# Routing by rank in a hybrid attention and mixture-of-experts layer: a shorter choice, moved splits, and reordered gathers and scatters

## The reference, cut to what matters

```python
g_prob = softmax(xt @ w_group + b_group)
g_w, g_idx = top_k(g_prob, 1)                      # one group per token
e_logits = take_along_axis(e_logits_all, g_idx)    # the 4 experts of that group
e_w, e_idx = top_k(softmax(e_logits), 2)           # two of them
e_w = e_w / sum(e_w)
w_tok = g_w[:, None] * e_w
for e in range(16):
    h = silu(xt @ w_gate[e]) * (xt @ w_up[e])
    y = y + combine[:, e:e + 1] * (h @ w_down[e])
x = layer_norm(ALPHA * x + y)
```

## Time and profile before

| | |
|---|---|
| median of 3 runs | 615.74 us (615.70 to 617.25) |
| profiled execution | 615.53 us |
| its span in the trace | 613.6 us |
| PE busy | 591.4 us (96%) |
| DVE busy | 478.5 us (78%) |
| ACT busy | 373.4 us (61%) |
| POOL busy | 129.3 us (21%) |
| share of PE in the chain that ended last | 92% |

### The profile page before, as it was taken

One profiled execution on the slowest core, in us unless ns is written; L12 is line 12 of the kernel. 1 busy time (PEld: TensorE's weight loads), 2 busy tenths in 40 slices (PEclk: granted clock), 3 DMA queues, 4 the chain that ended last, 5 costly groups with the idle time before them and its releaser, 6 DMA issues.

```text
span 613.6 us, 9635 instructions
## 1 busy us (share of the span) xinstructions
PE 591.4 (96%) x3627; PEld 475.8 (78%) x3627; DVE 478.5 (78%) x572; ACT 373.4 (61%) x401; POOL 129.3 (21%) x111
## 2 busy tenths in 40 slices
PE   8999999999999999999799999999999999999991
PEld 6878888888788668877588888888888888888880
DVE  3748598794577775546898989888888988888967
ACT  3659434431315984213478877877877787787745
POOL 0004222290000340000484443111110111111010
PEclk9999999999999999999899999999999999999997
DMA  9821133223306003975699999999999999999754
GB/s 325 299 98 57 63 130 111 95 71 78 72 1 206 2 2 125 422 271 211 239 375 420 404 363 389 392 388 391 409 404 389 389 389 389 399 410 397 269 172 137
DMA packets 42573, 155.77 MB, mean 254 GB/s; under 512 B 11955, under 2 KB 12163, under 8 KB 30252
## 3 DMA queue, kind: packets, MB, share of 16 engines
q1 hardware_dynamic: 37516, 138.40, 57.8%
q0 software_dynamic: 5024, 16.92, 10.6%
HBM read 139.96 MB, written 15.34 MB: 253 GB/s over the span
## 4 chain that ended last, share of the span: by engine, by line
PE 92%; DVE 4%; issue 1%; ACT 1%; DMA 1%; DVEq 0%; SPq 0%
PE psum L673 26%; PE psum L675 25%; PE psum L674 25%; PE psum L1072 2%; PE psum L791 2%; PE psum L931 2%; PE psum L908 2%; PE psum L1089 1%; PE psum L895 1%; PE psum L687 1%; DMA cst<-in_c_main 1%; PE psum L833 1%; PE psum L821 1%; PE psum L777 1%; DVE ring L2033 1%
## 5 line engine op out<-in xcount | busy, mean ns | idle before, releaser
L1810 DVE TENSOR_TENSOR w_lo<-ring,w_hi 128x2048 fp32r<-128x2048 f32 x95 | 216.8, 2299 | 23.3 <-ACT w_hi L1380 22.1
L673 PE MATMUL psum<-w_hi,act_hi 128*128 128x512 f32 x538 | 216.5, 402 | 0.8 <-DVE w_lo L1810 0.6
L675 PE MATMUL psum<-w_hi,act_lo 128*128 128x512 f32 x538 | 210.3, 391 | 0.0
L674 PE MATMUL psum<-w_lo,act_hi 128*128 128x512 f32 x538 | 210.0, 390 | 0.0
L1380 ACT ACTIVATE w_hi<-ring 128x2048 fp32r<-128x2048 f32 x96 | 182.2, 1917 | 25.0 <-PE psum L675 22.3
L673 PEld LDWEIGHTS psum<-w_hi,act_hi 128*128 128x128 f32 x538 | 101.3, 188 | 26.9 <-DVE w_lo L1810 4.7
L675 PEld LDWEIGHTS psum<-w_hi,act_lo 128*128 128x128 f32 x538 | 101.0, 188 | 21.9
L674 PEld LDWEIGHTS psum<-w_lo,act_hi 128*128 128x128 f32 x538 | 101.2, 188 | 19.0
L627 POOL DMA_INDIRECT acc_dram<-misc,slots x15 | 25.8, 1720 | 192.8 <-ACT misc L1430 178.8
L1228 ACT ACTIVATE w_hi<-ring 128x2048 fp32r<-128x2048 f32 x17 | 32.6, 1918 | 49.0 <-PE psum L675 47.3
L1539 DVE TENSOR_TENSOR w_lo<-ring,w_hi 128x2048 fp32r<-128x2048 f32 x17 | 39.8, 2344 | 23.0 <-ACT w_hi L1228 22.8
(11 more groups left out here) (254 smaller groups left out, 692.7 us busy)
## 6 DMA issues: line engine op xcount, KB each, us to landing
ring<-in_w_gate SPq DMA_DIRECT2D x32, 1024.0 KB, 19.8
ring<-in_w_up SPq DMA_DIRECT2D x32, 1024.0 KB, 19.6
ring<-in_w_down SPq DMA_DIRECT2D x32, 1024.0 KB, 19.9
ring<-in_w_in SPq DMA_DIRECT2D x13, 1024.0 KB
ring<-in_w_o SPq DMA_DIRECT2D x4, 1024.0 KB
acc_dram<-ring SPq DMA_DIRECT2D x5, 512.0 KB, 4.0
ring<-in_x SPq DMA_DIRECT2D x2, 1024.0 KB, 6.4
ring<-strip_dram SPq DMA_DIRECT2D x8, 256.0 KB, 4.9
```

Of the source, the lines that this page charges most:

```text
L673: pe.matmul(dst, lh, rh, start=first, stop=False, skip_group_check=True)
L674: pe.matmul(dst, lh, rl, start=False, stop=False, skip_group_check=True)
L675: return pe.matmul(dst, ll, rh, start=False, stop=last, skip_group_check=True)
L1810: dve.tensor_tensor(w_lo[:, v0 % WBUF, :], ring[:, slot, :], w_hi[:, v0 % WBUF, :].bitcast(F32), ALU.subtract).then_inc(s_lo, 1)
```

## The change

The choice by two rounds of "first maximum" is replaced by a rank: for every group of four values all 16 differences are compared with a small table (0 where the rival stands earlier, the smallest positive number otherwise), and the count of wins of the others is the rank. Rank 0 among the groups is the group; ranks 0 and 1 among the experts of it are the two choices. The ranks of tokens 0 to 255 are computed before the last tile's residual, the rest where the choice was. What served only the weights and addresses is put into two functions, `softmax_parts` and `records`, that stand later on DVE. Low parts 0 and 1 stand directly behind the first two indices, `overflow` moves behind low part 6, gathers 2 and 3 stand ahead of the eight scatters, ACT's exponential moves behind the split of expert 1's tokens, and PE's `keep_warm` counts change (32, 24 to 29, 9, 30). PE's first unit of expert 0 goes through its three products one after another instead of pairwise.

```diff
-    c[:, C_W4:C_W4 + 4] = [4, 3, 2, 1]
+    c[:, C_TIE:C_TIE + 16] = [0 if i < j else np.finfo(np.float32).tiny for j in range(4) for i in range(4)]
...
             pool.wait_ge(s_pads, 16 * (SEQ // P))
+            pool.wait_ge(s_slots, 3)
+            gather(2)
+            gather(3)
             pool.wait_ge(s_addr, 2)
             for n in range(2 * T):
-                if n == 5:
-                    pool.wait_ge(s_slots, 3)
-                    gather(2)
-                if n == 7:
-                    gather(3)
                 scatter_record(n)
...
-            keep_warm(32, 4)
+            keep_warm(29, 4)
             pe.wait_ge(s_pool, 4)
             pe.wait_ge(s_mask, 1)
...
             last.then_inc(s_pos, 1)
+            keep_warm(9, 1)
             pe.wait_ge(s_rec, 1)
...
-            keep_warm(24, 1)
+            keep_warm(30, 1)
             pe.wait_ge(s_xg[0], 16)
...
-            pe.wait_ge(s_lo, MIX_UNITS + 1)
-            block = lambda k: (slice(k * P, (k + 1) * P), slice(k * DE, (k + 1) * DE))
-            for k in range(4):
-                xs, ws = block(k)
-                high(bank(2), e_hi[:, 0, xs], w_hi[:, 0, ws], w_lo[:, 0, ws], k == 0)
-            pe.wait_ge(s_xtlofirst, 1)
...
+            pe.wait_ge(s_hi, MIX_UNITS + 1)
+            passes = [(e_hi, w_hi), (e_hi, w_lo), (e_lo, w_hi)]
+            for n, (x, w) in enumerate(passes):
+                if n == 1:
+                    pe.wait_ge(s_lo, MIX_UNITS + 1)
+                elif n == 2:
+                    pe.wait_ge(s_xtlofirst, 1)
+                for k in range(4):
+                    last = pe.matmul(bank(2), x[:, 0, k * P:(k + 1) * P], w[:, 0, k * DE:(k + 1) * DE], start=(n == 0 and k == 0), stop=False,
+                                     skip_group_check=True)
...
-            act.wait_ge(s_rneed, 1)
-            act.activation(r_x, r_x, ACT.Exp).then_inc(s_rexp, 1)
...
             xt_hi(1, 1)
+            act.wait_ge(s_rneed, 1)
+            act.activation(r_x, r_x, ACT.Exp).then_inc(s_rexp, 1)
             silu(0, 2, 0)
...
+            def ranks(t0):
+
+                ls = r_l[:, t0:t0 + 2, :].rearrange("p t (g e) -> p (t g) e", e=4)
+                shape = (P, 2 * (1 + NG), 4, 4)
+                link(dve.tensor_tensor(r_beats, ls.rearrange("p s (a i) -> p s a i", a=1).broadcast_to(shape),
+                                       ls.rearrange("p s (j a) -> p s j a", a=1).broadcast_to(shape), ALU.subtract))
+                tie = cst[:, C_TIE:C_TIE + 16].rearrange("p (a j i) -> p a j i", a=1, j=4)
+                link(dve.tensor_tensor(r_beats, r_beats, tie.broadcast_to(shape), ALU.is_ge))
+                link(dve.tensor_reduce(r_rank[:, t0:t0 + 2, :].rearrange("p t (g e a) -> p (t g) e a", e=4, a=1), r_beats, AX.X, ALU.add))
+
+            ranks(0)
             residual(T - 1, 1)
...
-            first_max(r_l, r_hot, r_top, r_first, T * (1 + NG))
-            link(dve.scalar_tensor_tensor(out=r_l2, in0=r_hot[:, :, NG:NL], scalar=-BIG, in1=r_l[:, :, NG:NL], op0=ALU.mult, op1=ALU.add))
-            first_max(r_l2, r_hot2, r_top2, r_first2, T * NG)
...
+            ranks(T // 2)
+            link(dve.tensor_scalar(r_group, r_rank[:, :, 0:NG], 0.5, None, ALU.is_lt))
...
-            link(dve.tensor_tensor(r_both, r_hot[:, :, NG:NL], r_hot2, ALU.add))
-            in_group(r_msk, r_both).then_inc(s_mask, 1)
+            dve.scalar_tensor_tensor(out=four(r_msk), in0=four(r_rank[:, :, NG:NL]), scalar=1.5, in1=group_four,
+                                     op0=ALU.is_lt, op1=ALU.mult).then_inc(s_mask, 1)
...
             elo(0, 0)
+            elo(1, 0)
...
+            def softmax_parts():
+
+                link(dve.tensor_reduce(r_top, r_l[:, :, 0:NG], AX.X, ALU.max))
+                link(dve.tensor_scalar(r_hot, r_rank[:, :, NG:NL], 0.5, None, ALU.is_lt))
+                link(dve.tensor_scalar(r_hot2, r_rank[:, :, NG:NL], 1.0, None, ALU.is_equal))
+                link(dve.tensor_tensor(r_x[:, :, 0:NG], r_l[:, :, 0:NG], bc(r_top, NG), ALU.subtract))
+                in_group(r_sel[:, 0], r_hot)
+                link(in_group(r_sel[:, 1], r_hot2))
+                link(dve.tensor_tensor(r_step, r_sel[:, 1], r_sel[:, 0], ALU.subtract))
+                link(dve.tensor_tensor(r_step, r_step, r_l[:, :, NG:NL], ALU.mult))
+                dve.tensor_reduce(r_x[:, :, NG:NG + 1], r_step, AX.X, ALU.add).then_inc(s_rneed, 1)
...
-            elo(1, 0)
             elo(2, 0)
             place(2)
             place(3)
             elo(3, 0)
+            softmax_parts()
             xt_lo(1, 1)
             slots_of(2, EARLY, 6)
             elo(4, 0)
-            overflow()
+            records()
             elo(5, 0)
             hidden(0, 4, 0)
             elo(6, 0)
+            overflow()
```

More of the change, by code:

```diff
@@ L66 @@
 C_SCAN = C_MASK + 64 * (1 + len(LEVELS))
-C_W4 = C_SCAN + SEQ
-C_E16 = C_W4 + 4
+C_TIE = C_SCAN + SEQ
+C_E16 = C_TIE + 16
 C_REC = C_E16 + NE
@@ L1869, in _ @@
             link(logits_of(T - 1))
[L1870 to L1884 removed]
+            ranks(T // 2)
+            link(dve.tensor_scalar(r_group, r_rank[:, :, 0:NG], 0.5, None, ALU.is_lt))
+            four = lambda v: v.rearrange("p t (g e) -> p t g e", g=NG)
+            group_four = r_group.rearrange("p t (g a) -> p t g a", a=1).broadcast_to((P, T, NG, EPG))
             def in_group(dst, src):
[L1887 to L1891 removed]
+                return dve.tensor_tensor(four(dst), four(src), group_four, ALU.mult)
+            dve.scalar_tensor_tensor(out=four(r_msk), in0=four(r_rank[:, :, NG:NL]), scalar=1.5, in1=group_four,
+                                     op0=ALU.is_lt, op1=ALU.mult).then_inc(s_mask, 1)
             dve.wait_ge(s_used, MIX_UNITS)
@@ L1921, in _ @@
-            in_group(r_sel[:, 0], r_hot[:, :, NG:NL])
-            in_group(r_sel[:, 1], r_hot2)
-            link(dve.scalar_tensor_tensor(out=r_pos, in0=pos, scalar=float(NE), in1=e16.broadcast_to((P, T, NE)), op0=ALU.mult, op1=ALU.add))
-            r_sel_flat, r_t16_four = r_sel, r_t16.rearrange("p (k i) e -> p k i e", k=2)
-            link(dve.tensor_tensor(r_t16_four, r_sel_flat, r_pos.rearrange("p (a i) e -> p a i e", a=1).broadcast_to((P, 2, T, NE)), ALU.mult))
-            link(dve.tensor_reduce(r_adr, r_t16, AX.X, ALU.add))
@@ new lines, in records @@
+            def records():
+                link(dve.scalar_tensor_tensor(out=r_pos, in0=pos, scalar=float(NE), in1=e16.broadcast_to((P, T, NE)), op0=ALU.mult, op1=ALU.add))
+                r_sel_flat, r_t16_four = r_sel, r_t16.rearrange("p (k i) e -> p k i e", k=2)
+                link(dve.tensor_tensor(r_t16_four, r_sel_flat, r_pos.rearrange("p (a i) e -> p a i e", a=1).broadcast_to((P, 2, T, NE)), ALU.mult))
+                link(dve.tensor_reduce(r_adr, r_t16, AX.X, ALU.add))
+                dve.tensor_copy(addr_i[:, :, :].rearrange("p k i -> p (k i)"), r_adr.rearrange("p n a -> p (n a)")).then_inc(s_addr, 1)
+                dve.wait_ge(s_rexp, 1)
+                link(dve.tensor_reduce(r_gsum, r_x[:, :, 0:NG], AX.X, ALU.add))
+                link(dve.tensor_scalar(r_q, r_x[:, :, NG:NG + 1], ALPHA, ALPHA, ALU.mult, ALU.add))
+                link(dve.tensor_tensor(r_gsum, r_gsum, r_q, ALU.mult))
+                link(dve.reciprocal(weight_of(rec_i[:, :, 0, 2:3]), r_gsum))
+                dve.tensor_tensor(weight_of(rec_i[:, :, 1, 2:3]), weight_of(rec_i[:, :, 0, 2:3]), r_x[:, :, NG:NG + 1], ALU.mult).then_inc(s_addr, 1)
```

31 lines of the change are left out of this document (3 added, 28 removed).

## The result

The changed kernel takes 620.05 us (median of 9 runs, 618.13 to 621.84) against 616.88 us of the kernel before on the same chip (9 runs, 615.70 to 618.61). The ratio is 1.0054 with a 95% interval of 1.0039 to 1.0069: 3.3 us slower, where 0.3% or 1.85 us is what such a comparison can tell from no change. The time is 0.65 us above the upper end of the forecast's range. The runs of before that the forecast started from had a median of 615.74, 1.1 lower. A ratio is taken over the runs of both kernels and is not the quotient of the two medians. The profiled execution took 621.65 us (span 619.8, 6.2 above that of before); it lies 1.6 above its kernel's median, while the profiled execution of before lies under all 9 of that kernel's runs.

A forecast was written before the change was run, and what follows sets the result against it. PE was taken to bound the kernel. Of 2.8 us gained in the opening 1.0 stayed; a 2.4 us wait for the table left 1.4, taken as 1.3: 615.74 + 1.3 = 617.0 us, range 614.0 to 619.4.

The forecast's parts named there:

- the wait ahead of L1088: Expert 0 on PE: a wait of 1 to 2 us, as PE comes 2.8 us earlier and `hidden` only 1.0.
- The choice, -1.88: Routing on DVE: the path to the mask instruction falls from 3.17 to 1.29 us, a gain of 1.88.
- The transposes "at 2.0 earlier": Start of expert 0 on PE: transposes start 2.0 us earlier, between 1.9 (the gather alone) and 2.3.
- should stay at 1.00: PE ahead of expert 0's transposes: nine new products fill the idle gap, so the granted clock stays at 1.00.
- What DVE gives back, 15.9: DVE from behind the token split to expert 0's `hidden`: 15.9 us instead of 14.85, leaving 1.0 of 2.8 gained.
- The scatters: POOL: about one scatter leaves per DVE low part, the last at 336.7, 8.4 us later than before.
- Landing and load, 5.5 + 5.4: Behind the last scatter: 5.5 us to land and 5.4 to load the table, weights at 347.9.
- L634, "0 to 0.8 on top": POOL's L634 (3.98 us) falls next to DVE's low parts and may hold one up, adding 0 to 0.8 us.
- The wait at `y_out`, 2.4: ACT at expert 1's `y_out`, due at 345.5, waits 2.4 us for the weights from the table.
- "I count the delay in full": Behind expert 1's `y_out`: ACT's delay passes on to DVE and PE, making the end 1.4 us later.
- Rivals 1 and 2: 1: scatters keep up, no wait, 614.7, chance 0.22. 2: opening gives 2.8 in full, no wait, 612.9, chance 0.09.
- Rival 3: Gather 0 on POOL is caught by low part 0, everything shifts by 2.3 us: 619.4 us, chance 0.14.

The follow-up runs named there:

- the constant weight and 44 fillers: Changed kernel with expert 1's weight the constant one and 44 instead of 30 keep_warm products ahead of expert 0's transposes: 616.33 us, ratio 0.9991.
- the constant weight: Changed kernel with expert 1's weight the constant one, copied on POOL ahead of the gathers: 616.71 us, ratio 0.9989.
- records early, gathers first: Changed kernel with softmax_parts and records ahead of the token split, low part 1 behind it, the exponential back in its old place: 617.76 us, ratio 1.0025.
- POOL's old order: Same as records early, gathers first, but gather 2 behind five scatters and gather 3 behind seven: 615.58 us, ratio 0.9985.
- POOL's order alone: Kernel before with only gathers 2 and 3 moved ahead of all eight scatters: 623.3 us, ratio 1.0104.
- the changed kernel with 44 fillers: Changed kernel with 44 instead of 30 keep_warm products ahead of expert 0's transposes: 619.84 us, ratio 1.0042.

## Why the prediction was wrong

Its mechanism held in outline: a shorter choice, given back by DVE, and then a table too late for expert 1. The time came out 3.05 us above the forecast of 617.0. Of this, 1.1 is the basis (before at 615.74 in its first 3 runs, 616.88 in the 9 that ran with the changed kernel); the difference to before was forecast at 1.3 and is 3.3, so 2.0 lie in the terms. In the trace `y_out` of expert 1 comes 4.1 us later than before (350.90 less 0.29, against 346.53) where 1.4 was forecast. Of these 2.7 us, 1.8 are the opening (`hidden` 0.9 later instead of 1.0 earlier) and 0.8 the table's landing and load. Another 1.5 follow that were counted as nothing. Of the signs it named, the mask, the clock from 297 to 301, the wait ahead of L1088 (1.65) and the scatters of 2 to 3 us came as said; ACT's idle time was 3.92 instead of 2 to 3.

- **The choice, -1.88**: measured -1.89 at the mask. The three instructions over 160 elements took 0.32 to 0.33 each, and the first half of the ranks lay in the idle time as said. Right.
- **The transposes "at 2.0 earlier"**: measured 1.4 (300.29 less 0.29, against 301.42). I had taken 4.24 us from start to landing as the gather's; it was 4.71 here, and 4.9 to 5.3 in the five other runs with the early gather and a view of its landing. The clock "should stay at 1.00" failed with it: PE idled 1.34 for the gather and then ran its first unit at 0.56 to 0.58. DVE then waited 1.98 us for high part 3 where 0.5 was counted. This step failed in the trace. The nine fillers closed one gap, and a new one opened a few us later.
- **What DVE gives back, 15.9**: measured 17.13 (302.88 to 320.01), with that wait 1.48 longer than counted. In the trace with the constant weight and 44 fillers, without the clock's fall, it was 15.5 (303.09 to 318.57), so the terms for the small instructions were right, and only the start was 1.1 later than the 302.0 I had. For `hidden` 1.0 earlier was forecast; 0.9 later it was, and 0.3 to 0.6 earlier with the longer filler (318.57 and 318.25).
- **The scatters**: the last left 18.8 us behind `hidden` in the forecast, 18.9 in the trace, each of 1.9 to 3.1 us but the sixth (332.51, 0.97), which met a split that reads PSUM and not a low part. The rule of one per low part was right, and so was the part that the order of issue plays. The Trainium skill's remark ("SBUF — State Buffer", "Who interferes with whom") that a tensor_tensor was not seen to stall a DMA does not hold for these scatters: they take 2.66 and 1.90 us in the rows shown, and with four fewer the last one left 9.6 us earlier, where free ones of 1.3 us would have made 5.2.
- **Landing and load, 5.5 + 5.4**: 5.12 and 6.60 (344.02 to 350.62), together 0.8 more than counted.
- **L634, "0 to 0.8 on top"**: 0 in the changed kernel, where the low parts beside it take their usual 4.49. It is real elsewhere: 7.64 instead of 6.90 for three low parts in the kernel before, 5.79 instead of 4.49 for two with the constant weight.
- **The wait at `y_out`, 2.4**: 3.17 in the trace, by the 0.8 of landing and load. **"I count the delay in full"** stands for the step that the sum left out, what comes behind the wait. In the trace it is 1.5 us between the two `y_out`, with PE's idle 3.07 us and a clock of 0.84. The trace with the old choice and all the moves has a wait of 3.76, PE idle 2.91, a clock of 1.00, and nothing on top (18.14 between the two). So the 1.5 is what the clock took in this execution, not what every such wait costs, and buffers that come free later add nothing to it there. Why the clock fell in one and not in the other is not shown.

The medians give the price of a wait by pairs that differ in it and little else. The limits are estimates from the two intervals. The last column is PE's idle time for DVE's slowed low parts in the run without the wait (L634, above); it is missing in the run with it, so the price is too low by up to that much.

| pair | wait beyond the usual 0.75 | price by the ratios | to be added, at most |
|---|---|---|---|
| changed kernel, the same with constant weight | 3.17 | 4.0 (2.7 to 5.3) | 1.19 |
| the two with 44 fillers | 3.11 | 3.1 (2.0 to 4.3) | 1.06 |
| records early, gathers first or POOL's old order | 3.14 | 2.5 (1.3 to 3.7) | 0.49 |
| POOL's order alone, the kernel before | 5.91 | 6.4 (5.4 to 7.5) | 0 |

So a wait costs at least about its length. Whether it costs a microsecond more on the average, as the clock's fall in the trace would have it, the medians leave open.

In the medians, then: everything but the wait -0.7 (the constant weight against the kernel before; forecast -1.0), the wait +4.0 (forecast +2.4), sum +3.3. The failed term is the wait. Its table came 0.8 us later by landing and load than counted, and nothing was counted for what follows it. The opening failed too (transposes 2.0 earlier, clock at 1.00), by 1.8 us in the trace, but the medians hardly bear that out: the filler that mends it brings 0.7 (-0.6 to 2.1).

Rivals 1 and 2 fell (the scatters did not keep up, and the opening did not give 2.8). Rival 3 did not take place: gather 0 took 1.05 us in all executions. It named the time nearest to the result (619.4), by a mechanism that did not act.

What stays open is why a gather that starts at 295.2 to 295.5 takes 4.7 to 5.3 us to land, and one that starts at 296.8 to 297.0 takes 4.2. In the window 294 to 298 the DMA engines moved 265 GB/s in the changed kernel and 203 in the kernel before, so weight transfers may be in its way; no run varied them. Also open is what decides in an execution whether the clock falls, ahead of the mask product or behind the wait.

## What to carry to other kernels

A queue that only supplies something later still has a due date: before its items are reordered, count how many of them fall under the other engine's long instructions, since a held item costs that engine's spacing (2.4 us here) and not its own length (1 us). A gain at the start of a stretch is worth only what the engines behind it let through, here 1.0 (0.2 to 1.8) of 1.9 us with the choice alone. When a wait appears on the path, count its length in full and look in the trace for what the clock does behind it: here 1.5 us more in one execution and nothing in another. A run that removes a wait can let another engine's work fall somewhere new; compare the instructions' durations on both sides before its time is read as the price of the wait.

## What the runs showed of the hardware that was not expected

- An indirect DMA on POOL that meets a low part of DVE (float32, 128 x 2048, two operands in SBUF) takes 1.9 to 3.1 us instead of 1.0, in every run, and ends some 0.85 us behind that low part. One that starts beside a split with one operand in PSUM takes 0.97 (332.51 in the changed kernel, the split from 331.77 to 332.99).
- It works the other way too. POOL's multiplication of 128 x 1024 (L632) beside low parts made two of them 5.79 and 5.65 us long instead of 4.49, and three 7.62 to 7.87 instead of 6.9.
- The spread between executions of one kernel goes with the clock. In the 12 runs of the changed kernel with 44 fillers, mean granted clock and time correlate at -0.97, 0.7 us for 0.001 of clock (0.987 to 0.993); in the changed kernel it is -0.79 and 0.6 us, and the weakest is -0.46 with the constant weight. That is about what 0.1% of the whole time is. Which of the two comes first, the lower clock or PE's idle time, such a number does not say.
- Idle times of PE of 1.3 to 2.0 us ahead of the transposes were each followed by a clock of 0.50 to 0.71 between 302 and 306; with the filler that closes them (44 products) it was 1.00. One execution (constant weight) had an idle time of 0.88 and kept 1.00. Behind the late table, idle times of 3.01 to 3.07 in three traces were followed by a clock of 0.50 to 0.72, and one of 2.91 was not.
- Eight small scatters take 4.8 to 5.4 us to be seen as landed behind the last one where both gathers go ahead of them, and 6.6 to 7.0 where a gather stands between the seventh and the eighth. The load of the 128 x 48 table then takes another 5.1 to 5.6 us from its issue where it is issued at 332 to 338 (or 2.7 us behind a gather), and 6.4 to 7.0 where it is issued at 342 to 345. What makes the difference was not varied.
